# Moving three jobs of the mixer from VectorE to GpSimd: the low parts of twelve weight groups, the attention tables, and the output bias

## The reference

```
xn = RMSNorm(x) * g_mix
a, g, q, k, v = split(xn @ w_in + b_in)            # 5 parts of 512 columns
conv = silu(LayerNorm(depthwise_conv31(a * sigmoid(g))))
attn = neighbourhood_attention(q, k, v, rpb)       # 8 heads, window 8 x 16
h = x + concat(conv, attn) @ w_out + b_out
h = h + MoE_top4_of_32(RMSNorm(h))
out = RMSNorm(h)
```

## Time and profile before

| | us |
|---|---|
| three runs | 1546.91, 1549.3, 1551.53 |
| median | 1549.3 |
| the profiled execution | 1546.91, with a span of 1545.1 |
| mean granted TensorE clock of the profiled execution | 0.951 |

### The profile page before, as it was taken

How to read it: one execution, slowest core, us unless ns; L and a number is a source line. 1 busy time by engine, 2 the same in 40 slices (tenths; PEclk the granted TensorE clock), 3 DMA queues, 4 the chain that set the end, 5 groups by cost and what they waited for, 6 DMA issues and landing times.

```text
span 1545.1 us, 19165 instructions
## 1 busy us (share of the span) xinstructions
PE 1425.8 (92%) x6484; PEld 1165.6 (75%) x6484; DVE 1303.2 (84%) x1008; ACT 960.3 (62%) x708; POOL 248.5 (16%) x212
## 2 busy tenths in 40 slices
PE   4997599946999999999999999999999999999993
PEld 3885257645788888888888888888888888888873
DVE  6599834267899999999999999999999999999996
ACT  3231342133677777777777777777777777777761
POOL 2000730041111111111111111111111111111162
PEclk9999679956999999999999999999999999999997
DMA  7930200184899999999999999999999999999972
GB/s 256 342 98 26 90 1 1 34 298 185 306 377 384 381 391 388 393 388 378 382 385 394 375 386 386 377 401 391 381 377 388 391 377 393 379 383 391 386 285 93
DMA packets 84913, 479.54 MB, mean 310 GB/s; under 512 B 10667, under 2 KB 10966, under 8 KB 35734
## 3 DMA queue, kind: packets, MB, share of 16 engines
q1 hardware_dynamic: 71918, 433.40, 72.4%
q0 software_dynamic: 6944, 25.18, 4.7%
q10 hardware_dynamic: 6024, 20.60, 3.4%
HBM read 449.82 MB, written 29.33 MB: 310 GB/s over the span
## 4 chain that ended last, share of the span: by engine, by line
PE 80%; DVE 6%; SPq 4%; issue 4%; DMA 2%; ACT 2%; POOL 1%; DVEq 1%; POOLq 0%; ACTq 0%
PE pair L1685 22%; PE pair L1683 22%; PE pair L1684 22%; SPq L453 2%; PE pair L1696 2%; PE pair L1663 2%; PE pair L1670 2%; DVE area_m L1029 2%; PE pair L1541 1%; PE pair L1560 1%; PE pair L1502 1%; DMA h<-in_x 1%; SPq L443 1%; PE pair L1504 1%; PE pair L1503 1%
## 5 line engine op out<-in xcount | busy, mean ns | idle before, releaser
L1194 DVE TENSOR_TENSOR w_low<-w_raw,w_high 128x2048 fp32r<-128x2048 f32 x377 | 857.6, 2292 | 95.5 <-ACT w_high L816 93.5
L816 ACT CAST w_high<-w_raw 128x2048 fp32r<-128x2048 f32 x380 | 728.0, 1917 | 280.7 <-PE pair L1685 280.7
L1683 PE MATMUL pair<-w_high,xT_high 128*128 128x512 f32 x1040 | 409.3, 394 | 0.0
L1685 PE MATMUL pair<-w_high,xT_low 128*128 128x512 f32 x1040 | 406.8, 391 | 0.0
L1684 PE MATMUL pair<-w_low,xT_high 128*128 128x512 f32 x1040 | 406.0, 390 | 0.0
L1685 PEld LDWEIGHTS pair<-w_high,xT_low 128*128 128x128 f32 x1040 | 196.0, 188 | 41.6
L1684 PEld LDWEIGHTS pair<-w_low,xT_high 128*128 128x128 f32 x1040 | 196.2, 189 | 40.3
L1683 PEld LDWEIGHTS pair<-w_high,xT_high 128*128 128x128 f32 x1040 | 196.3, 189 | 39.9
L1683 PE MATMUL pair<-w_high,hT_high 128*128 128x512 f32 x496 | 195.6, 394 | 0.0
L1684 PE MATMUL pair<-w_low,hT_high 128*128 128x512 f32 x496 | 193.1, 389 | 0.0
L1685 PE MATMUL pair<-w_high,hT_low 128*128 128x512 f32 x496 | 193.1, 389 | 0.0
(11 more groups left out here) (296 smaller groups left out, 1436.1 us busy)
## 6 DMA issues: line engine op xcount, KB each, us to landing
w_raw<-in_w_gate SPq DMA_DIRECT2D x128, 1024.0 KB, 7.0
w_raw<-in_w_up SPq DMA_DIRECT2D x128, 1024.0 KB, 6.3
w_raw<-in_w_down SPq DMA_DIRECT2D x128, 1024.0 KB, 6.9
y_rows<-area_m ACTq DMA_DIRECT2D x30, 512.0 KB
ring<-in_w_in SPq DMA_DIRECT2D x5, 2048.0 KB, 17.9
y_rows<-area_t SPq DMA_DIRECT2D x1, 8704.0 KB
ring<-in_w_out SPq DMA_DIRECT2D x2, 2048.0 KB, 8.2
h<-in_x SPq DMA_DIRECT2D x4, 512.0 KB
```

Of the source, the lines that this page charges most:

```text
L816: s.copy(w_high[:, i % HIGH_RING, :], w_raw[i][:, :]).then_inc(high_ready, 1)
L1194: v.tensor_tensor(w_low[i][:, :], w_raw[i][:, :], w_high[:, i % HIGH_RING, :].bitcast(F32), ALU.subtract).then_inc(low_ready, 1)
L1683: t.matmul(to[half], tok_high, hi, start=(opens and kk == 0), stop=False)
L1685: last = t.matmul(to[half], tok_low, hi, start=False, stop=(k == KD - 1))
```

## The change

1. The low parts of groups 8 to 19 are made by GpSimd, in the order of the groups, counted by a new semaphore `win_low_pool`. TensorE waits for that count in place of `win_low_dve`.
2. All 24 table adds are made by GpSimd, behind these low parts and ahead of the low parts of `w_out`.
3. `b_out` is loaded once as a row broadcast to 128 partitions, by ScalarE's queue behind the xnT copies. GpSimd adds it to `h` in four adds of 128x1024, ahead of everything else named here, counted by `xb_ready`. The load on 64 partitions, its two splitting steps and the eight opening matmuls go away. ScalarE waits for `xb_ready` ahead of the kT copies (the row lies in their place), and VectorE ahead of attention.
4. VectorE's conv taps now run without anything between them except `glu`; SyncE issues the first three expert pieces, not two, right after the last load of `w_out`.

```diff
-        bout_raw = ring[0:64, 4, 2048:3072]
-        bout_rows = over("bout_rows", ring_at, 4 * 4096 + 3072, [64, D_MODEL])
+        bout_row = area_k[:, 1024:2048]
...
-            sp.dma_start(bout_raw, bass.AP(b_out.tensor, b_out.offset, [[0, 64], [1, D_MODEL]])).then_inc(bout_loaded, 16)
-            for i in range(2):
+            for i in range(3):
                 load(i, 0)
...
+            pool.wait_ge(bout_loaded, 16)
+            for n in range(NQ):
+                pool.wait_ge(xn_ready, n + 1)
+                g.tensor_tensor(h[:, n, :], h[:, n, :], bout_row, ALU.add).then_inc(xb_ready, 1)
+
+            for g_i in range(8, 20):
+                loaded, high, low = split_parts(g_i)
+                pool.wait_ge(win_high_ready, g_i + 1)
+                g.tensor_tensor(low, loaded, high.bitcast(F32), ALU.subtract).then_inc(win_low_pool, 1)
+
+            pool.wait_ge(mask_step, 13)
+            pool.wait_ge(y_stored, 16)
+            pool.wait_ge(proj_done, 8)
+
+            for hd in range(HEADS):
+                pool.wait_ge(raw_loaded, 16 * N_ROWS * (hd // 2 + 1))
...
+                    g.tensor_tensor(dst.rearrange("p (m r c) -> p m r c", r=N_ROWS, c=QB), src,
+                                    mask[:, o:o + w].rearrange("p (m r c) -> p m r c", r=N_ROWS, c=QB),
+                                    ALU.add).then_inc(tables_ready, 1)
...
+            act.dma_start(bout_row, row_bcast(b_out, D_MODEL)).then_inc(bout_loaded, 16)
...
+            act.wait_ge(xb_ready, NQ)
...
-            s.activation(bout_rows[:, :], bout_raw, ACT.Copy, scale=16.0).then_inc(bout_high, 1)
...
             glu(2)
-            win_low_part(8)
-            conv_taps(0, 6, 9)
+            conv_taps(0, 6, 13)
             glu(3)
-            at = 9
-            for g in range(9, 20):
-                win_low_part(g)
-                if g % 2 and g < 17:
-                    tables((g - 9) // 2 * 2)
-                    tables((g - 9) // 2 * 2 + 1)
-                conv_taps(0, at, at + 2)
-                at += 2
+            conv_taps(0, 13, CONV_K)
             conv_start(2)
             conv_taps(2, 1, CONV_K)
-            dve.wait_ge(bout_high, 1)
-            v.scalar_tensor_tensor(bout_rows[32:64, :], bout_raw[32:64, :], 16.0, bout_rows[32:64, :].bitcast(F32),
-                                   ALU.mult, ALU.subtract).then_inc(bout_split, 1)
...
             dve.wait_ge(tables_ready, 3 * HEADS)
+            dve.wait_ge(xb_ready, NQ)
...
             for g in range(16):
-                pe.wait_ge(win_low_dve, g + 1)
+                if g < 8:
+                    pe.wait_ge(win_low_dve, g + 1)
+                else:
+                    pe.wait_ge(win_low_pool, g - 7)
...
-            pe.wait_ge(win_low_dve, 20)
+            pe.wait_ge(win_low_pool, 12)
...
-                if not attn:
-                    t.matmul(bank[OUT_BANKS[half]][:, :], mean_w[0:64, :].bitcast(F32R), bout_rows[:, half * HALF:(half + 1) * HALF],
-                             start=True, stop=False)
```

More of the change, by code:

```diff
@@ L271, in encoder_kernel @@
         bout_loaded = sem("bout_loaded")
-        bout_high = sem("bout_high")
-        bout_split = sem("bout_split")
         stage_loaded = sem("stage_loaded")
@@ L294, in encoder_kernel @@
         win_low_dve = sem("win_low_dve")
+        win_low_pool = sem("win_low_pool")
         stage_transposed = sem("stage_transposed")
@@ L297, in encoder_kernel @@
         bq_ready = sem("bq_ready")
+        xb_ready = sem("xb_ready")
         proj_done = sem("proj_done")
@@ L470, in _ @@
             sp.dma_start(unit(6), wout_v[:, :, 0:HALF]).then_inc(wout_loaded[0], 16)
-            sp.dma_start(bout_raw, bass.AP(b_out.tensor, b_out.offset, [[0, 64], [1, D_MODEL]])).then_inc(bout_loaded, 16)
-            for i in range(2):
+            for i in range(3):
                 load(i, 0)
             sp.wait_ge(wout_done, 2 * NQ)
-            for i in (2, 3, 4):
+            for i in (3, 4):
                 load(i, 0)
@@ L559, in _ @@
                 rstd_of(n, ss_ready)
+            pool.wait_ge(bout_loaded, 16)
[11 more added lines that the diff above has]
+                pool.wait_ge(raw_loaded, 16 * N_ROWS * (hd // 2 + 1))
+                raw = raw_bias[:, hd % 2, :].rearrange("p (r w) -> p r w", r=N_ROWS)
+                for kind, (dst, m0, m1, o) in enumerate(((T_mid[:, hd, :], 0, 3, 0), (T_edge[:, hd, 0, :], 1, 3, 384),
+                                                         (T_edge[:, hd, 1, :], 0, 2, 640))):
+                    w = (m1 - m0) * P
+                    src = raw[:, :, m0 * QB:m1 * QB].rearrange("p r (m c) -> p m r c", c=QB)
+                    g.tensor_tensor(dst.rearrange("p (m r c) -> p m r c", r=N_ROWS, c=QB), src,
+                                    mask[:, o:o + w].rearrange("p (m r c) -> p m r c", r=N_ROWS, c=QB),
+                                    ALU.add).then_inc(tables_ready, 1)
             for c in range(4):
@@ L737, in _ @@
                 wout_high_part(1, c)
-            act.wait_ge(bout_loaded, 16)
-            s.activation(bout_rows[:, :], bout_raw, ACT.Copy, scale=16.0).then_inc(bout_high, 1)
             for c in range(CC):
@@ L1030, in conv_taps @@
                                                mixedT[:, c, :], ALU.mult, ALU.add).then_inc(conv_tap, 1)
[L1032 to L1046, removed]
             for g in range(4):
@@ L1498, in _, with three_products @@
             pe.wait_ge(cols_ready, 1)
-            def three_products(to, a_high, a_low, b_high, b_low, k, opened=False):
-                t.matmul(to, a_high, b_high, start=(k == 0 and not opened), stop=False)
+            def three_products(to, a_high, a_low, b_high, b_low, k):
+                t.matmul(to, a_high, b_high, start=(k == 0), stop=False)
                 t.matmul(to, a_high, b_low, start=False, stop=False)
@@ L1579, in project_out @@
                 else:
-                    pe.wait_ge(bout_split, 1)
                     pe.wait_ge(conv_low_ready, CC)
@@ L1591, in project_out @@
                         high, low = conv_high[:, k, tokens], conv_low[k][:, tokens]
-                    last = three_products(bank[OUT_BANKS[half]][:, :], high, low, wout_high[half][:, k, :], wout_low[half][:, k, :], k, opened=True)
+                    last = three_products(bank[OUT_BANKS[half]][:, :], high, low, wout_high[half][:, k, :], wout_low[half][:, k, :], k)
                 if attn:
```

## The result

The changed kernel takes 1561.1 us (median of five, 1559.64 to 1563.63) against 1548.9 for the kernel before (five, 1546.91 to 1551.53). The ratio is 1.0083, 95% interval 1.0069 to 1.0096: it is slower by 12.3 us, not by 28.2. The profiled execution took 1556.89 us with a span of 1555.1.

The account below looks back on a forecast made before the run. VectorE's list of low parts, tables and 124 taps was taken to hold the mixer's end. LayerNorm start +31.6 and removed matmuls -3.4 gave +28.2, on the median of 1549.3 the forecast 1577.5 us, range 1564 to 1589.

Parts of the forecast that it names:

- Groups 10 to 19: Low parts stuck behind VectorE's gapless taps to 144.8, TensorE standing still from 87.5; LayerNorm start +31.6 us.
- rival C: Waiting GpSimd instructions get in after one tap each, stretching VectorE's taps; LayerNorm +20, in all 1566; chance 0.06.
- The tables: Table adds on GpSimd behind the low parts end at 207.4, VectorE asks at 210.1: hidden by 2.7, bounds 0 and +4.
- The loads of `w_out`: First half's load, asked for at 204, wanted by ScalarE 9 us after LayerNorm starts: hidden.
- The removed matmuls: Eight matmuls of 0.43 us leave the chain that ended last: -3.4 us, the only gain reaching the end.
- VectorE's list: Relieved of low parts, table adds and a 3.25 us step, VectorE's list would end some 27 us earlier, near 142.5.
- Groups 8 and 9: Their low parts get in on GpSimd at `glu(2)` and `glu(3)`; no cost for group 8, margin about 0.5 us for 9.
- The bias row: Loaded by some 32 to 36, its four GpSimd adds done before 47; cost 0.
- Rival B: GpSimd gets in at conv_start at 104, group 10 ready at 106, total 1573.5; chance 0.10.
- The mean: TensorE's matmuls right after the v product, at the full clock, taken as 3.5 us ahead of the LayerNorm start.

Follow-up runs that it names:

- e4: The changed kernel with SyncE's first load of `w_out` issued ahead of the third pair's table loads; 1550.82 us, ratio 1.0016.
- e1: The kernel before with only part 3 of the change, `b_out` added to `h` by GpSimd and no opening matmuls; 1541.97 us, ratio 0.9964.
- e2: The changed kernel with the table adds back on VectorE between the taps, low parts still on GpSimd; 1549.26 us, ratio 1.0011.
- e6: The changed kernel with small memsets keeping GpSimd busy while it waits for table loads; 1559.91 us in one run.
- e8: e1 with eight small GpSimd adds released at set tap counts in the taps of blocks 2 and 3; 1541.61 us in one run.
- e5: The changed kernel with three one-column VectorE copies from PSUM between stretches of seven turns of the last taps; 1561.65 us, ratio 1.0084.
- e9: e1 with taps 9 to 30 of blocks 0 and 1 in one loop, five GpSimd adds in it, low parts 9 to 19 behind; 1556.59 us, one run.
- e3: The changed kernel with the low parts of groups 8 to 19 back on VectorE between taps, tables still on GpSimd; 1546.56 us, ratio 0.9988.

## Why the prediction was right in its direction and wrong in its size

The forecast was +28.2, of it +31.6 ahead of the LayerNorm start and -3.4 behind it. On the ruler it came to +12.5: +3.2 in stretch A, 28.4 less than forecast, and +9.3 in stretch B, 12.7 more. So two steps failed, in opposite directions, and the second hid part of the first. That the sign came out right owes more to the load of `w_out`, which the sum left out, than to the stand-still that it was built on.

- **Groups 10 to 19** is the step that failed: "taps issued without a gap never let GpSimd in", "Nothing on GpSimd moves, so TensorE stands still from 87.5", +31.6 at the LayerNorm start. Measured from the first `glu` it was +3.2, and TensorE did not stand still. The rule was read from one instance, the 19.52 us of the earlier trace rows. In the loop of blocks 0 and 1 GpSimd, once it had got in beside `glu(3)` at 75.19, kept its turn after each tap. That is rival C, to which I gave 0.06. Its mechanism and nearly its price for VectorE are what the 36 taps show: 49.96 - 23.9 = 26.1 us, of which the ten low parts of groups 10 to 19 make 10 x (2.8 - 0.66) = 21.4, the end of group 9 about 1, and the first six table adds the rest. Only the tables did not add the 18.6 it asked for, since most adds of the third pair and all of the fourth ran behind the taps. Each of these low parts stood ready when the one before it had just held up a tap; the subtraction of the earlier trace rows came 75 us after VectorE had last stood still (more on this at the end).
- **The tables, hidden by 2.7.** In the new order they are not hidden. The third pair was stuck for 33 us and VectorE waited 5.96 us for the fourth. With the load of `w_out` out of the way (e4) the whole change comes to +2.6, the gain of the bias part taken off.
- **The loads of `w_out`** are the second step that failed, and the largest single loss: 10.3 us (e4). There are two. The sum has a term only for the one that SyncE issues second (its "first half's load", asked for at 204 when the v product is done), whose four casts stand 9 us behind the LayerNorm start: "hidden". The one that it issues first, behind all table loads, is in no term, and its four casts stand in ScalarE's list ahead of the LayerNorm squares. By the prediction's own dates the table loads end near 200.7; with the 7.90 us from issue to landing and the 3.88 of the casts the squares begin at 212.5, not 0.7 behind the LayerNorm start at 208.3, a term of +4 that the sum did not have. Measured, it was 10.3, since the third pair's add was stuck to the end of the taps.
- **The removed matmuls, -3.4.** Right in kind; e1 measured -4.3 in stretch B and -6.2 in the median.
- **VectorE's list, "some 27 us earlier, near 142.5".** The 27 counts the 3.25 us step, which stands behind the last tap and moves it by nothing. The 142.5 holds even so, since the new order fills the 4.65 us of idle time ahead of `glu(3)`, which the list of savings leaves out.
- **Groups 8 and 9.** The price for TensorE was right, nothing. Group 9 went in at `glu(3)` as foreseen; group 8 was earlier than I had it and got in ahead of conv_start, at 54.36, which then took 3.08 us in place of 1.
- **The bias row.** Right: adds from 30.95 to 43.4. Most of that lies ahead of the ruler, but there TensorE waited for no low part, and in e1 the first `glu` starts at 44.31, before at 43.99; stretch A of e1 is 0.4 us longer.
- **Rival B's point**, whether conv_start is an opening. It is: the add of 121.38 got in before the conv_start of 126.39, which was held for it (2.12 us, not 0.99). So a GpSimd add that has begun holds a conv_start as it holds a tap. The Trainium skill states the same exclusion for a VectorE instruction in a two-port mode (SBUF — State Buffer, "SBUF: two separate sides"), and these rows agree with it.
- **The mean** took 6.00 us, not 3.5, since TensorE had paused for 31.29 ahead of it and was at the lower of its two clock levels for most of it (granted 0.61 in 170.5 to 176.5, before 0.55 in 169.3 to 175.9).

Of the 12.3 us: the bias part -6 (e1), the low parts on GpSimd with the new order of the taps +7 (e2 against e1), the tables on GpSimd +11 (after against e2), of which 10 is the load behind them (e4). The third early expert piece was not tried by itself.

## What to carry to other kernels

Work with two SBUF inputs moved from VectorE to GpSimd beside more such work on VectorE brought nothing here: either VectorE stands still for GpSimd's duration, which is about twice its own (2.37 against 1.21 us), or GpSimd is stuck. So relieve VectorE only where its other work reads PSUM or where it is idle. Before a chain is moved to a slower or starvable engine, list what stands behind its waits in each in-order queue, DMA queues among them, and what stands behind that on the engine that waits for it: one load in SyncE's queue was worth 10 us here. An exclusion seen once says how long the two hold each other, not who is next. And look for pauses in the list of the engine that others wait for: filling the 4.65 us ahead of `glu(3)` gave, with the bias part, the lowest median, 0.5% below the kernel before.

## What the runs showed of the hardware that was not expected

Beside VectorE's gapless taps a waiting GpSimd instruction met one of two fates. Either the engines took strict turns, one instruction each, or it got nothing until the loop was over: 19.52 us before, 33.15 after, 33.13 in e6, 38.87 in e8, each with own durations of 0.7 to 2.4. A VectorE copy with its input in PSUM ended the second at once (e5).

Neither the loop nor GpSimd's idle time decides. In the changed kernel the add of 121.38 waited 5 us in the loop of blocks 0 and 1, in which e9 admitted all; in e5 a subtraction arrived in the taps of blocks 2 and 3 (there in stretches of 14) and had its turn after one tap, its four instructions taking 10.77 us (POOL):

```profile
162.54 10.77 POOL L588 TENSOR_TENSOR wout_low<-ring,wout_high 128x1024 fp32r<-128x1024 f32 x4 [0.23 <-ACT wout_high L759]
```

What goes with the fate in all stretches of taps alone is how long VectorE had run without a stop when the instruction arrived, a stop being idle time or an instruction held up by GpSimd:

| arrival | VectorE without a stop for, us | what happened |
|---|---|---|
| e5, 162.54 | 0.23 | next turn |
| after, 97.45 | 2.13 | next turn |
| e9, the five adds | 1.35 to 3.34 | next turn |
| after, 121.38 | 5.41 | waits to the end of the loop |
| after, 138.17 | 5.36 | 33.15 |
| e6, 141.14 | 5.37 | 33.13 |
| e5, 141.21 | 5.43 | waits to the copy from PSUM |
| e8, 133.16 | 52.1 | 38.87 |
| before, 151.96 | 75.4 | 19.52 |

The traces of the other runs have no exception in such stretches. It fits the kernel too: the low parts follow each other closely, while each pair of tables arrives 5.4 us after the last, because its load begins only when the pair before is done. Two things limit the reading. No run varies this time alone, and between 3.34 and 5.36 us there is no arrival. And in e3, where a low part stands between every four taps, adds that arrived 5.4 us after the last stop got in within two instructions. What in the engines is behind it stays open.
